# Squares of two norms summed on GpSimd, K and V cleared group by group, and each norm's last products moved one block on

## What is computed

```python
def rmsnorm(x, g):
    y = x * rsqrt(mean(x * x, axis=-1) + EPS)
    return y * g

x = x + 0.5 * ((silu(gate) * up) @ w_out)         # gate, up = split(rmsnorm(x, norm_ffn1) @ ffn1_w_in)
h = rmsnorm(x, norm_mix)                          # "n2" in the kernel
u, q, k, v, ga, gb = split(h @ w_in)
ya = multiscale_pool(u)                           # branch A, windows 2/4/8/16
yb = sliding_window_attention(rmsnorm(q), rmsnorm(k), v, sinks)
x = x + (sigmoid(ga) * (ya @ w_pool_proj) + sigmoid(gb) * (yb @ w_attn_proj)) @ w_out
x = x + half_swiglu(rmsnorm(x, norm_ffn2))        # "n3" in the kernel
```

## Time and profile before

| | |
|---|---|
| median of 3 runs | 1475.67 us (1475.35 to 1476.4) |
| the profiled execution | 1477.62 us, of which the slowest core's span is 1476.6 us |
| spans of the eight cores | 1467.9 to 1476.6 us |
| busy, slowest core | TensorE 1437.0 us, VectorE 621.7, ScalarE 393.1, GpSimd 138.1 |

### The profile page before, as it was taken

The page is one execution under the profiler, slowest core; times in us unless marked ns, Lnnn a source line. Parts: engine busy times, 40 slices in busy tenths (PEclk is TensorE's granted clock), DMA queues, the critical chain, the costliest instruction groups (busy, mean ns, idle before and its releaser), DMA issues.

```text
span 1476.6 us, 23995 instructions; the slowest of 8 cores (1467.9 to 1476.6 us)
## 1 busy us (share of the span) xinstructions
PE 1437.0 (97%) x8341; PEld 790.1 (54%) x8341; DVE 621.7 (42%) x1200; ACT 393.1 (27%) x651; POOL 138.1 (9%) x214
## 2 busy tenths in 40 slices
PE   5999999999999999998999999999999999999998
PEld 2455555555555455554776555555555555555554
DVE  2445225323522485555666344474262262243235
ACT  5530110111011355556555222343101101101110
POOL 2000000000000045561000000000000000000000
PEclk9899999999999999999999999999999999999999
DMA  9732230231011241215111731205304104200014
GB/s 225 167 61 52 39 62 15 37 63 30 1 29 29 79 200 26 23 29 83 27 30 30 204 83 29 79 16 101 72 15 72 30 15 71 44 1 1 1 35 201
DMA packets 43957, 88.86 MB, mean 60 GB/s; under 512 B 25504, under 2 KB 27168, under 8 KB 42560
## 3 DMA queue, kind: packets, MB, share of 16 engines
q0 software_dynamic: 18128, 57.32, 21.3%
q1 hardware_dynamic: 25712, 30.01, 6.1%
HBM read 114.97 MB, written 18.38 MB: 90 GB/s over the span
## 4 chain that ended last, share of the span: by engine, by line
PE 92%; POOL 2%; issue 2%; DVE 2%; ACT 1%; DMA 1%; DVEq 0%; POOLq 0%; ACTq 0%
PE ps L512 44%; PE ps L564 21%; PE ps L1029 4%; PE ps L1096 4%; PE ps L1080 4%; PE ps L1075 4%; PE ps L856 3%; PE ps L1039 2%; PE ps L988 2%; PE ps L947 1%; PE ps L453 1%; PE ps L792 1%; DMA X<-xin 1%; DVE hT L467 1%; PE ps L1016 0%
## 5 line engine op out<-in xcount | busy, mean ns | idle before, releaser
L512 PE MATMUL ps<-hT,ring 128*128 128x448 bf16 (+2 forms) x3536 | 656.0, 349 | 6.0 <-DVE hT L467 6.0
L512 PEld LDWEIGHTS ps<-hT,ring 128*128 128x128 bf16 x3536 | 348.0, 98 | 311.8 <-issue 12.4
L520 DVE TENSOR_TENSOR Abuf<-ps,sl 128x448 bf16<-128x448 f32 (+2 forms) x221 | 134.2, 609 | 499.4 <-PE ps L512 459.2
L564 PE MATMUL ps<-Abuf,Wo 128*128 128x448 bf16 (+1 forms) x1760 | 330.9, 347 | 0.0
L519 ACT ACTIVATE sl<-ps 128x448 bf16<-128x448 f32 (+2 forms) x221 | 116.8, 531 | 740.6 <-PE ps L512 738.6
L564 PEld LDWEIGHTS ps<-Abuf,Wo 128*128 128x128 bf16 x1760 | 172.2, 98 | 151.0
L568 DVE SCALAR_TENSOR_TENSOR X<-ps,X 128x448 f32<-128x448 f32 (+1 forms) x320 | 195.3, 611 | 115.9 <-PE ps L564 114.0
L397 POOL DMA_DIRECT2D ring<-wst x71 | 38.0, 537 | 947.0 <-PE ps L512 625.7
L467 DVE SCALAR_TENSOR_TENSOR hT<-X,colv,rstd 128x448 bf16<-128x448 f32 (+1 forms) x112 | 72.5, 675 | 15.4 <-ACT rstd L464 14.7
L856 PE MATMUL ps<-hT,ring 128*128 128x448 bf16 (+1 forms) x320 | 63.8, 348 | 4.4 <-DVE ya L835 2.5
L1029 PE MATMUL ps<-hT,ring 128*128 128x448 bf16 (+1 forms) x320 | 65.1, 347 | 2.3 <-ACT tg L1031 2.3
(11 more groups left out here) (108 smaller groups left out, 848.7 us busy)
## 6 DMA issues: line engine op xcount, KB each, us to landing
ring<-wst POOLq DMA_DIRECT2D x63, 512.0 KB, 5.2
Wo<-wo POOLq DMA_DIRECT2D x12, 768.0 KB, 8.9
xsp<-X SPq DMA_DIRECT2D x5, 1792.0 KB, 5.7
X<-xsp SPq DMA_DIRECT2D x5, 1792.0 KB, 18.0
X<-xin POOLq DMA_DIRECT2D x8, 896.0 KB, 30.3
y_out<-X SPq DMA_DIRECT2D x6, 896.0 KB, 3.6
ring<-wst POOLq DMA_DIRECT2D x8, 384.0 KB, 8.0
Wo<-wo POOLq DMA_DIRECT2D x4, 512.0 KB, 5.2
```

What stands on the lines that cost most here:

```text
L512: P.pe(lambda: T.matmul(ps[:, bks[x][half], 0:n], lhsT=w[:, kc, 128 * half:128 * half + 128], rhs=hT[:, kc, c0s[g] + o_:c0s[g] + o_ + n], ...
L520: P.dve(lambda: V.tensor_tensor(out=Abuf[:, jj, c0s[g] + o_:c0s[g] + o_ + n], in0=ps[:, bu, 0:n], in1=slt[i][:, 0:n], op=ALU.mult), r=[ban ...
L564: P.pe(lambda: T.matmul(ps[:, bk, 0:n], lhsT=Wo[b][:, jj, 128 * m:128 * m + 128], rhs=Abuf[:, jj, c0s[g]:c0s[g] + n], start=(jj == 0), sto ...
```

## The change

It does four things.

- For n2 and n3 the squares of slices 0 to 6 are added on GpSimd (six additions per group: f32 in between, bf16 at the last), and two products per group remain, of the sum and of the last square. The pair is issued by `tick(0)` behind the next block's matmuls instead of two blocks later; after the last group, behind the next stage's first. n2 has tiles of its own for rstd. In the last output projection of FFN 1 `drain(1)` is left out for slices 3 and 7.
- kT and Vb are cleared seven chunks at a time, for group 0 in front of the mixer and for group g + 1 behind group g. The operation of GpSimd that follows a clear waits for it.
- `next_step` drains one hT instead of two, and the mixer starts when hT of group 2 has been issued.
- In groups 0 to 3 the four U come in the order 0, 1, 2, 3 instead of 3, 2, 1, 0, and ya's claims on X2 and X3 are taken apart by window.

```diff
@@ norm_sq @@
-        lagq.append(mm)
+        if x:
+            lagq.append(mm)
+            return
+        if key == "n3":
+            ac, rac = accL, r_sl[0:2]
+            ab, rab = (accB, r_accB) if g % 2 == 0 else (accM, r_sl[2])
+        else:
+            ac, rac = accF, [r_acc] + r_sqx[0:2]
+            ab, rab = accN[g % 2], r_accb[g % 2]
+        if kc == 0:
+            sqp[g] = (t, rt)
+        elif kc < KC - 1:
+            src, rsrc = (sqp[g][0], [sqp[g][1]]) if kc == 1 else (ac, rac)
+            dst, rdst = (ab, [rab] + ([] if key == "n3" else r_sqx[2:4])) if kc == KC - 2 else (ac, rac)
+            P.gps(lambda: G.tensor_tensor(out=dst[:, 0:n], in0=src[:, 0:n], in1=t[:, 0:n], op=ALU.add), r=rsrc + [rt], w=rdst,
+                  extra=ng_["sq"])
+        else:
+            def mm2():
+                P.pe(lambda: T.matmul(ps[:, sbk, 0:n], lhsT=cb[:, 0, :], rhs=ab[:, 0:n], start=True, stop=False),
+                     r=[rab, r_cb], w=[bank[sbk]])
+                P.pe(lambda: T.matmul(ps[:, sbk, 0:n], lhsT=cb[:, 0, :], rhs=t[:, 0:n], start=False, stop=True),
+                     r=[rt, r_cb], w=[bank[sbk]])
+                norm_fin(key, g, lo, n, gcol, sbk)
+            lagq.append(mm2)
@@ out_proj @@
-                drain(1)
+                tick(0)
+                if not last or m % 4 != 3:
+                    drain(1)
                 if last and gcol_next is not None:
                     norm_sq(next_key, g, m, lo[g], n, gcol_next)
-                tick(2)
@@ behind FFN 1 @@
-    need_h("n2", NG - 2)
-    P.gps(lambda: G.memset(kT[:], 0.0), w=all_K + rX[0] + rX[1])
-    P.gps(lambda: G.memset(Vb[:], 0.0), w=all_V + rX[1] + rX[2])
-    for p in range(2):
-        P.gps(lambda p=p: G.memset(Vb[64 * p:64 * p + 64, :, :, p, 64:65].rearrange("k c h o -> k (c h) o"), 1.0), w=all_V, extra=[P.last["pool"]])
+    mguard = P.guard()
+
+    def kv_clear(g):
+        P.gps(lambda: G.memset(kT[:, :, 7 * g:7 * g + 7, :, :], 0.0), w=[r for a in r_K[g] for r in a] + rX[0] + rX[1])
+        vw = [r for b in r_V[g] for d in b for r in d]
+        P.gps(lambda: G.memset(Vb[:, 7 * g:7 * g + 7, :, :, :], 0.0), w=vw + rX[1] + rX[2])
+        for p in range(2):
+            P.gps(lambda p=p: G.memset(Vb[64 * p:64 * p + 64, 7 * g:7 * g + 7, :, p, 64:65].rearrange("k c h o -> k (c h) o"), 1.0), w=vw,
+                  extra=[P.last["pool"]])
+        P.fence = [P.last["pool"]]
@@ next_step @@
-        drain(2)
+        drain(1)
@@ the mixer's groups @@
-    need_h("n2", 0)
-    mguard = P.guard()
+    need_h("n2", 2)
+    kv_clear(0)
...
-            seq = [K, Vv(0, 1), U(3), Q(0), Vv(2, 3), Q(1), U(2), Q(2, 3), Q(3), U(1), Q(4, 2), Q(5), U(0), Q(6, 1), Q(7, 0)]
+            seq = [K, Vv(0, 1), U(0), Q(0), Vv(2, 3), Q(1), U(1), Q(2, 3), Q(3), U(2), Q(4, 2), Q(5), U(3), Q(6, 1), Q(7, 0)]
...
+        if g + 1 < NG:
+            kv_clear(g + 1)
```

More of the change, by code:

```diff
@@ L60, in __init__ @@
         self.nops = 0
+        self.fence = []
     def add(self, eng, fn, reads=(), writes=(), dma=False, extra=(), sig=True):
@@ L146, in gps @@
     def gps(self, fn, r=(), w=(), **k):
+        if self.fence:
+            k["extra"] = list(k.get("extra", ())) + self.fence
+            self.fence = []
         return self.add("pool", fn, r, w, **k)
@@ L279, in build @@
         vtm.append(t)
+    mfree = e
+    rst2 = []
+    for i in range(2):
+        t, e = at("rstn%d" % i, [128, GW], F32, e)
+        rst2.append(t)
+    mend = m0 + 8 * TM * 2 + 4 * KC * GW * 2
+    accB, e = at("accB", [128, GW], BF16, mend)
+    e = m0 + (6 * TOK + 12 * D) * 2
+    accF, e = at("accF", [128, GW], F32, e)
+    accN = []
+    for i in range(2):
+        t, e = at("accN%d" % i, [128, GW], BF16, e)
+        accN.append(t)
+    assert e <= mfree
+    e = scr + NSQ * 2 * GW
+    accL, e = at("accL", [128, GW], F32, e)
+    accM, e = at("accM", [128, GW], BF16, e)
     e = x_off
@@ L321, in build @@
     r_sl = [R("sl%d" % i) for i in range(3)]
+    r_acc, r_accb, r_accB = R("accF"), [R("accN0"), R("accN1")], R("accB")
+    r_rst2 = [R("rstn0"), R("rstn1")]
     r_rst = [R("rst%d" % i) for i in range(2)]
@@ L439, in build @@
     ng_ = {"sq": ()}
+    sqp = {}
+    rst_, r_rst_ = rst, r_rst
     def norm_sq(key, g, kc, lo, n, gcol, x=False):
@@ L456, in mm @@
                 norm_fin(key, g, lo, n, gcol, sbk)
-        lagq.append(mm)
-    def norm_fin(key, g, lo, n, gcol, sbk):
-        i = cnt["rst"] % 2
-        cnt["rst"] += 1
+        if x:
[22 more added lines that the diff above has]
+            lagq.append(mm2)
+    def norm_fin(key, g, lo, n, gcol, sbk):
+        if key == "n2":
+            i = g % 2
+            rst, r_rst = rst2, r_rst2
+        else:
+            i = cnt["rst"] % 2
+            cnt["rst"] += 1
+            rst, r_rst = rst_, r_rst_
         P.act(lambda: S.activation(out=rst[i][:, 0:n], in_=ps[:, sbk, 0:n], func=AF.Ln, bias=cv_[:, C_EPS:C_EPS + 1]),
@@ L783, in build, with ya_x @@
     ya_f = []
+    def ya_x(g, cg):
+        if cg == 0:
+            return []
+        assert g or ("n2", 3) in h_done
+        return rX[3]
     def step_u(g, cg):
@@ L813, in step_u @@
             out=ya[:, cg, m0_:m0_ + nm], in0=s_[:, 16:16 + nm], scalar=1.0 / wdt, in1=b[:, cg, 16:16 + nm],
-            op0=ALU.mult, op1=ALU.subtract), r=[rs_, rb], w=[r_ya[g][cg]] + rX[2] + rX[3]))]))
+            op0=ALU.mult, op1=ALU.subtract), r=[rs_, rb], w=[r_ya[g][cg]] + (rX[2] if cg < 2 else []) + ya_x(g, cg)))]))
         if g == NG - 1:
```

## The result

The changed kernel takes **1499.34 us** (median of 4 runs, 1498.41 to 1500.82), the kernel before 1475.63 in the same comparison: a ratio of 1.0162 (95% interval 1.015 to 1.0174). The prediction was 1476.3 us with a range up to 1483.5; it was 23 us too low.

What follows compares the result with a forecast made beforehand. TensorE was taken as the bound, at 92% of the chain. From 1477.6 us, less 4.9, 1.3 and 2.0, plus 5.2 and 3.6, came 1478.2, so 1476.3 for the median; range 1469.5 to 1483.5.

Steps and rivals of the forecast that it cites:

- What bounds the kernel: Whole kernel: TensorE carries 92% of the chain that ended last; another engine matters only where it makes TensorE stand still.
- n3, -4.9 us: w_out projection: fewer products save 5.3 us, 0.4 us charged for the pair's waits, so 4.9 us gained.
- n2, -1.3 us: FFN 1's last projection: 54.0 us becomes 52.7, with 5.8 us of stops; between a gain of 4.5 and a loss of 4.
- rival B: FFN 1's last projection: GpSimd becomes the bound, 3 us stops at four boundaries, 1481.6 us, up to 1485; chance 0.30.
- Rival A: Groups 2 and 4: the clears' cost is hidden, the products' gain kept; 1468 us, halfway 1472; chance 0.29.
- Rival C: FFN 1's last projection: an add keeps hT out for its whole 0.95 us instead of 0.72; 1478.3 us; chance 0.05.
- Group 0, -2 us: Mixer's group 0: 22.2 us becomes about 20.2 as the stop behind hT goes; gain between 0 and 3.5 us.
- Group 2, +5.2 us: Mixer's group 2: ya comes 4.0 us later behind GpSimd's queue, plus a lower clock; between +2.5 and +7 us.
- Group 4, +3.6 us: Mixer's group 4: GpSimd's chain starts 3.6 us later behind U(3) and the clear; between +2 and +5.5 us.
- The clock: Group 2: a lower clock behind TensorE's stop costs 1.76 us, as behind the 2.02 us stop in group 0.
- The sum: Whole kernel: the terms give 1478.2 us for the profiled execution, 1476.3 us for the median of the runs.

Runs made afterwards that it cites:

- n3_only: Kernel before with only the changed n3 (squares summed on GpSimd); n2, clears and mixer as before: ratio 0.9955, 1468.4 to 1469.4 us.
- n2_lag: Changed kernel with the old U order in groups 1 and 3, n2's pair behind the next group's second block instead of its first: 1471.0 us, ratio 0.9967.
- n2_dummy: Kernel before plus changed n3 and mixer (old U order in groups 1 and 3), with n2's six additions made but unused, eight products kept: 1473.35 us, ratio 0.9985.
- mix_only: Kernel before with only the change's clears, drains and U order; n2 and n3 as before: ratio 1.0067, mostly 1480.2 to 1482.3 us.
- after_again: The changed kernel itself, six more runs: 1483.05 to 1487.69 us without the long low-clock stretch, 1496.91 with it; ratio 1.0074.
- n3_split: Kernel before plus changed n3 and mixer (old U order in groups 1 and 3), samples' setup cut in three behind group 2's U(0), U(1), U(2): ratio 0.9926.
- stop2: Kernel before with four unneeded memsets on GpSimd ahead of the samples' setup in group 2: ratio 1.0024, median 1477.57 us.

## Why the prediction was wrong, point by point

- **What bounds the kernel.** Right: every loss can be named as a time for which TensorE stood or ran slower.
- **n3, -4.9 us.** Right: 63.9 to 58.9 us, and 59.0 in n3_only. No wait on a sum shows there; with 1.51 us blocks and few operations of VectorE the sum is in time.
- **n2, -1.3 us: the step that failed.** It became +4.9 us. The mechanism, a pair that waits for a sum which meetings of hT and additions make late, was that of the working; its sizes were not. (1) The stops were put at 0.6, 2.2, 1.5 and 1.5 us, 5.8 together; they were 0.92, 4.70, 1.72 and 2.01, 9.35. The price of one meeting for hT was about right (0.72 us forecast; 0.73 found at 506.79, 0.25 to 0.87 over the stage); for the addition it was too high (0.53 forecast, 0.11 to 0.48 found). Too small was the addition (0.95 us taken from one of 461 columns of f32, 1.04 found for 448) and with it the step of the chain, 1.09 against 1.18 us by itself and 1.39 beside hT. Far too small was the second boundary, 4.70 instead of 2.2: X comes 2 us late behind the hT that waits for Ln and Exp, in the kernel before too, and with the meetings VectorE no longer makes that up before the sum is due; 0.7 us had been added for it. (2) The lower clock behind a stop was priced in group 2 and not here: 2.5 us. Together 3.5 + 2.5 is the miss of 6 us. In price it is **rival B**, named with 1.4 us from start to start as the point from which it decides; 1.39 is what the chain shows. I had given the adds that meet nothing too much weight as evidence against it. In shape it is not quite B: one stop of the four reached its 3 us, and n2_lag, with the same additions and one block more of room, took the stops down to 5.2 us, so GpSimd's time for six additions is not what bounds the stage. What B did not say, n2_dummy showed: with eight hT a group 4 us are lost even where nobody waits for the sum, because VectorE becomes the bound.
- **Rival A**, the clears hidden, fell: the idle time of GpSimd that it counted on was too short, and the stages of groups 2 and 4 grew by 5.8 and 3.6 us.
- **Rival C** did not decide: no meeting cost hT the whole 1.04 us, the dearest 0.87. The Trainium skill's rule (SBUF — State Buffer, "SBUF: two separate sides") speaks of a lock for the whole instruction. By that rule the trace agrees: each long hT ends 0.47 to 0.49 us behind the addition's end. What the prediction had wrong was to read from it a fixed price of a whole addition; hT starts up to 0.8 us into one, and its first 0.2 us pass beside it.
- **Group 0, -2 us.** Right in sum, 20.1 against 20.2, in part by luck. The pair cost 1.84 us (1.68 and 0.16) instead of 1.1, and the further hT nothing instead of 0.7: without the pair, in mix_only, the stage took 18.3 us. On most cores of before, though, this stage took 20.8 us, not 22.2: the profiled core alone had the lower clock there, so for the kernel the gain is only 0.7 us. Taking the terms from one core hid that.
- **Group 2, +5.2 us.** Right in place and size: ya waits 9.79 us (about 10 forecast), TensorE 5.84 (5.9), the stage +5.8, with a lower clock behind it (1.4 us on 8 matmuls, 1.76 forecast).
- **Group 4, +3.6 us.** Right in size, +3.6, but by luck. The chain starts later as forecast; the stop sits at another place, and on core 2 1.5 us of the 3.6 are the lower clock, which the forecast had only in its range. Core 6 went through this group within the long stretch and took the same 32.7 us.
- **The clock.** The prediction took 1.76 us for what follows a stop. That a pair of cores may later stay at 0.81 for 161 us, and cost 17 us, was in neither the sum nor a rival; no row of before shows it. This is the larger half of the miss. With it left out (1483 to 1488 us in after_again) the change would still have ended at the upper end of the range or above it.
- **The sum.** From 1478.2 for the profiled execution: +6.2 (n2), +0.6 (group 2), +17.1 (clock), less 3.8 us that this core happened to be ahead, gives 1498.3; it was 1498.41.

## What to carry to other kernels

Before work is moved to GpSimd to save TensorE a fifth of a microsecond, count VectorE's operations with two SBUF inputs beside it: here thirty additions cost more than the thirty products that they replaced had, and only where VectorE has room (n3) did the move pay. A sum that another engine finishes wanted one block more of distance here than a clean chain suggests. And a stop of TensorE can have a second price, in clock, which is paid after it. Cut in pieces between other work (n3_split), the samples' setup cost no stop at all.

## What the runs showed of the hardware

- A GpSimd addition that reads f32 and bf16, or bf16 twice, takes 1.03 to 1.04 us for 448 columns, start to start 1.18 when each needs the one ahead; the earlier trace rows had 0.95 and 1.09 for 461 columns of f32.
- Beside a GpSimd addition hT takes 0.92 to 1.54 us instead of 0.67, and the addition 1.14 to 1.51 instead of 1.04; each ends a fixed time behind the other's end (hT 0.47 to 0.49 us, the addition 0.88 to 0.90). X's update, with one SBUF input, stays at 0.61 to 0.63. Beside memsets hT is as if alone (674 to 686 ns).
- A stop's length alone doesn't tell whether the clock falls behind it. In one trace (stop2) a stop of 2.47 us lost it on core 2 and one of 2.47 us kept it on core 4; in the one before 2.02 us lost it on core 6 and 2.02 to 2.03 us kept it on the seven others; 2.95 us kept it in n2_lag on cores 1 and 4 and lost it on core 2. Every stop of over 3.9 us in FFN 1's last projection and the mixer's groups lost it.
- The granted clock can be 0.81 on a pair of cores for 161 us, through group 4 and most of the scores, and return to 1.00 with no change in the work. What sets it off is open.
